# A transformer pair in split float32: where the SBUF buffers lie, with the two ends of the memory exchanged

## The chip, the cores and the metric

The kernel runs on 1 core of a Trainium2 chip. The metric is the time of one execution on the device, in microseconds. Before the change it is 1691.29 us, the median of 3 runs (1683.52 to 1696.0).

## What is computed

Two blocks run one after the other on 512 positions of width 1024, all in float32. The first block has three mixers side by side (an attention with forget gates of 8 heads, a windowed mean, a "stick-breaking" attention of 4 heads). The second block has two layers: a matrix memory (mLSTM) and an attention over a window of 128 with sinks, each followed by a layer norm, a squared-ReLU MLP, a layer norm and a gated side input. Cut to the MLP and the side input, in which the operands stand that this text is about:

```python
def squared_relu_mlp(x, w_up, w_down):
    return jnp.square(jax.nn.relu(x @ w_up)) @ w_down
...
        x = layer_norm(DEEPNORM_ALPHA * x + mix, mix_ln_g[i], mix_ln_b[i])
        x = layer_norm(DEEPNORM_ALPHA * x + squared_relu_mlp(x, mlp_w_up[i], mlp_w_down[i]), mlp_ln_g[i], mlp_ln_b[i])
        x = x + jax.nn.sigmoid(x @ ple_w_gate[i] + ple_b_gate[i]) * (p[i] @ ple_w_proj[i])
```

`w_up` is 1024 x 4096, `w_down` 4096 x 1024; the other weight matrices are 1024 wide as well.

## The kernel before

Activations lie transposed: features on the 128 partitions, the 512 positions along the free axis. A matrix of 1024 features is eight slices of 128 x 512 float32, that is 2048 bytes per partition and slice.

Every product with a weight matrix is made from halves. A number is split into a high part (rounded to the type `fp32r`) and the low rest, and three matmuls add up in one PSUM bank: high weight by high activation, low weight by high activation, high weight by low activation. The weights come in 238 blocks of 128 x 1024 float32 (4096 bytes per partition; the stationary operand of one matmul is a piece of 128 columns, 512 bytes per partition). For each block SyncE issues one DMA into `W_raw` (2 slots, L428), GpSimd writes `W_hi` (L445) and `W_lo` (L447), 4 slots each, and TensorE runs 8 x 3 matmuls with it. The inner lines of `product`, which all phases share, are

```python
pe.matmul(PS[:, bank, :], W_hi[:, slot, w], hi[:, kk, :], start=first, stop=False)      # L515
pe.matmul(PS[:, bank, :], W_lo[:, slot, w], hi[:, kk, :], start=False, stop=False)      # L516
done = pe.matmul(PS[:, bank, :], W_hi[:, slot, w], lo[:, kk, :], start=False, stop=last)  # L517
```

The second argument is the stationary operand (loaded by LDWEIGHTS, "PEld" in the profile), the third the moving one, 512 columns long. L485, L486 and L490 are the same three products in `weave`, with which some phases begin, and L825 to L827 are those of the small side product. The moving operand is one of three pairs:

- `A_hi`, `A_lo`: the split activations of 1024 features, in almost every phase;
- `H_hi`, `H_lo`: the 2048 hidden features of half an MLP, in the four `down` phases (8 tiles of 2 blocks each);
- `P_hi`, `P_lo`: the side input, in the two `proj` phases (8 tiles of a quarter block each).

The order of the work is written out by hand, engine by engine, with semaphores. ScalarE reads the banks out of PSUM (or VectorE does, for the residual sums in `X`), ScalarE writes the high parts and VectorE the low parts (`low_part`, L1297; `H_lo`, L1608). `GpSimd` may overwrite a weight slot when TensorE is done with it (the wait ahead of L444, a dummy operation on `HOLD`).

Buffers are allocated by `sb`, as on a stack. Each has a fixed byte address within the partition; those of a `with ... as part` or `sub` block are given back at its end, so that the buffers of the stages (`QK`, `MQK`, `QK3`, `H_hi`, `GATE` and so on) share their memory. Before the change the long-lived buffers are stacked from byte 16512 upwards in the order of the code, and the shared part stands above them, from 137760 up to 222432.

Of the kernel before, what the change touches and what calls it, by code (L numbers as in the profile page):

```python
# [19 lines left out]
F32 = mybir.dt.float32  # L20
F32R = mybir.dt.float32r
# [6 lines left out]
P = 128  # L28
T = 512
NT = T // P  # L30
D = 1024
KD = D // P
# [137 lines left out]

def build(nc, x, weights, constants, params, positions, ple_in, out):
    with ExitStack() as ctx:
        def sb(name, shape, dt=F32, where=ctx):
            return where.enter_context(nc.sbuf_tensor(name, shape, dt))

        def sem(name):
            return ctx.enter_context(nc.semaphore(name))


        X = sb("X", [P, KD, T])  # L180
        A_hi = sb("A_hi", [P, KD, T], F32R)
        A_lo = sb("A_lo", [P, KD, T], F32R)
        W_raw = sb("W_raw", [P, RAW_SLOTS, KD * P])
        W_hi = sb("W_hi", [P, W_SLOTS, KD * P], F32R)
        W_lo = sb("W_lo", [P, W_SLOTS, KD * P], F32R)
# [1703 lines left out]
```

## Time and profile before

| what | value |
|---|---|
| median of 3 runs | 1691.29 us |
| the profiled execution: its time, its span | 1691.69 us, 1689.5 us |
| TensorE busy | 1610.2 us, 95% of the span |
| GpSimd busy | 900.8 us, 53% |
| VectorE busy | 728.7 us, 43% |
| ScalarE busy | 424.5 us, 25% |
| mean DMA rate | 78 GB/s |
| mean granted TensorE clock | 0.987 of the full clock |

TensorE's busy time in this table is the union of matmuls whose ends are modelled, and one matmul's end lies behind the start of the next. How long TensorE takes for a matmul in a running stream is therefore read from the distance of two starts, or from a stretch of time divided by the number of matmuls in it, and not from the "mean ns" of a row. A stretch can lack some matmul records.

### The profile page before, as it was taken

What the parts mean: (1) busy time and instruction counts of PE and PEld (TensorE: products, weight loads), DVE (VectorE), ACT (ScalarE), POOL (GpSimd) and SP (SyncE); (2) the same over time, 40 slices, a digit from 0 to 9 for tenths busy, and PEclk for the clock granted to TensorE, in tenths of its full rate; (3) what the DMA queues carried; (4) which work ended last, traced back from release to release, by engine and by line L of the source; (5) the groups of instructions that cost most, each with busy time, mean ns of one, the idle gap of its engine ahead of it and who ended that gap; (6) DMA issues with size and microseconds to landing.
All of it is one profiled execution on the core that took longest, in us unless ns stands there. A gap on an engine that the chain in (4) does not pass through costs nothing.

```text
span 1689.5 us, 20635 instructions
## 1 busy us (share of the span) xinstructions
PE 1610.2 (95%) x7306; PEld 1280.2 (76%) x7306; DVE 728.7 (43%) x985; ACT 424.5 (25%) x916; POOL 900.8 (53%) x719
## 2 busy tenths in 40 slices
PE   5999998989999999999999999998999999999998
PEld 4788665778777778887888877777778888887876
DVE  5773243241103657500552154656576610453155
ACT  3321356221120132200220041147423200121041
POOL 4666300456542249766676646830156866676643
PEclk9999999999989999999999999999999999999999
DMA  4322100122311023332323213310022332333322
GB/s 156 100 88 88 62 1 13 53 85 94 93 50 50 13 88 100 100 100 88 100 91 108 90 59 100 100 51 0 13 88 75 104 96 90 97 100 100 99 76 75
DMA packets 36835, 132.34 MB, mean 78 GB/s; under 512 B 4105, under 2 KB 4385, under 8 KB 36770
## 3 DMA queue, kind: packets, MB, share of 16 engines
q1 hardware_dynamic: 35282, 128.23, 24.2%
q10 hardware_dynamic: 1488, 3.17, 0.5%
q8 instruction: 50, 0.82, 0.2%
q14 instruction: 15, 0.12, 0.0%
HBM read 129.26 MB, written 2.10 MB: 78 GB/s over the span
## 4 chain that ended last, share of the span: by engine, by line
PE 91%; ACT 3%; DVE 3%; issue 1%; DMA 1%; POOL 0%; SPq 0%; ACTq 0%; DVEq 0%; POOLq 0%
PE PS L515 23%; PE PS L517 23%; PE PS L516 23%; PE PS L485 2%; PE PS L490 2%; PE PS L486 2%; PE PS L630 2%; PE PS L601 2%; PE PS L770 1%; PE PS L617 1%; DMA W_raw<-in_weights 1%; ACT PR L1050 1%; PE PS L745 1%; PE PS L757 1%; PE PS L704 1%
## 5 line engine op out<-in xcount | busy, mean ns | idle before, releaser
L447 POOL TENSOR_TENSOR W_lo<-W_raw,W_hi 128x1024 fp32r<-128x1024 f32 x238 | 601.5, 2527 | 19.9
L515 PE MATMUL PS<-A_hi,W_hi 128*128 128x512 f32 x1176 | 468.0, 398 | 7.5 <-DVE A_lo L1297 3.7
L444 POOL TENSOR_TENSOR HOLD<-HOLD 1x1 f32<-1x1 f32 x238 | 60.2, 253 | 750.7 <-PE PS L517 458.8
L517 PE MATMUL PS<-A_lo,W_hi 128*128 128x512 f32 x1176 | 459.8, 391 | 0.0
L516 PE MATMUL PS<-A_hi,W_lo 128*128 128x512 f32 x1176 | 459.8, 391 | 0.0
L515 PEld LDWEIGHTS PS<-A_hi,W_hi 128*128 128x128 f32 x1176 | 222.1, 189 | 60.2 <-issue 8.6
L516 PEld LDWEIGHTS PS<-A_hi,W_lo 128*128 128x128 f32 x1176 | 222.2, 189 | 49.0 <-issue 3.6
L517 PEld LDWEIGHTS PS<-A_lo,W_hi 128*128 128x128 f32 x1176 | 221.8, 189 | 46.7
L445 POOL TENSOR_SCALAR W_hi<-W_raw 128x1024 fp32r<-128x1024 f32 x238 | 247.2, 1038 | 0.0
L515 PE MATMUL PS<-H_hi,W_hi 128*128 128x512 f32 x512 | 203.4, 397 | 2.7 <-ACT RELU L1180 2.7
L517 PE MATMUL PS<-H_lo,W_hi 128*128 128x512 f32 x512 | 203.0, 396 | 0.0
L516 PE MATMUL PS<-H_hi,W_lo 128*128 128x512 f32 x512 | 203.0, 396 | 0.0
L1608 DVE TENSOR_TENSOR H_lo<-SQR,H_hi 128x512 f32 (+1 forms) x64 | 122.4, 1913 | 57.4 <-ACT H_hi L1183 57.4
L1180 ACT ACTIVATE RELU<-PS 128x512 f32<-128x512 f32 x64 | 37.9, 592 | 322.2 <-PE PS L517 310.9
L1606 DVE TENSOR_TENSOR SQR<-RELU 128x512 f32<-128x512 f32 x64 | 81.3, 1270 | 85.9 <-ACT RELU L1180 85.9
L515 PEld LDWEIGHTS PS<-H_hi,W_hi 128*128 128x128 f32 x512 | 96.4, 188 | 27.8 <-ACT RELU L1180 4.4
L517 PEld LDWEIGHTS PS<-H_lo,W_hi 128*128 128x128 f32 x512 | 96.4, 188 | 23.5
L516 PEld LDWEIGHTS PS<-H_hi,W_lo 128*128 128x128 f32 x512 | 96.5, 188 | 23.3
L1555 DVE TENSOR_TENSOR X<-X,PS 128x512 f32<-128x512 f32 x32 | 22.0, 688 | 188.8 <-PE PS L517 188.8
L1552 DVE SCALAR_TENSOR_TENSOR X<-X,PS 128x512 f32<-128x512 f32 x24 | 16.4, 687 | 186.2 <-PE PS L517 177.6
L485 PE MATMUL PS<-A_hi,W_hi 128*128 128x512 f32 x168 | 69.2, 412 | 15.1 <-DVE MIX L1698 3.8
L1160 ACT ACTIVATE SQ<-X 128x512 f32<-128x512 f32 x28 | 17.7, 633 | 205.6 <-DVE X L1555 182.3
(247 smaller groups left out, 1807.5 us busy)
## 6 DMA issues: line engine op xcount, KB each, us to landing
W_raw<-in_weights SPq DMA_DIRECT2D x238, 512.0 KB, 3.5
X<-in_x SPq DMA_DIRECT2D x4, 512.0 KB, 6.1
out<-X ACTq DMA_DIRECT2D x8, 256.0 KB, 2.8
RELU<-in_ple_in ACTq DMA_DIRECT2D x2, 512.0 KB, 3.6
CONST<-in_constants SPq DMA_DIRECT2D x1, 913.5 KB, 10.8
PARAM<-in_params SPq DMA_DIRECT2D x1, 197.5 KB, 3.8
CONST<-in_constants SPq DMA_DIRECT2D x1, 192.0 KB, 7.6
NEG_C<-FF_PART ACTq DMA_DIRECT2D x3, 8.0 KB
```

Source lines behind the costliest of these rows:

```text
L444: pool.tensor_tensor(HOLD[:, 1 + s:2 + s], HOLD[:, 0:1], HOLD[:, 0:1], ALU.add)
L445: pool.tensor_scalar(W_hi[:, s, :], W_raw[:, r, :], 1.0, 1.0, ALU.mult, ALU.mult).then_inc(w_hi, 1)
L447: pool.tensor_tensor(W_lo[:, s, :], W_raw[:, r, :], W_hi[:, s, :].bitcast(F32), ALU.subtract).then_inc(w_lo, 1)
L485: pe.matmul(PS[:, i, :], W_hi[:, slot, w], hi[:, k, :], start=k == 0, stop=False)
L486: pe.matmul(PS[:, i, :], W_lo[:, slot, w], hi[:, k, :], start=False, stop=False)
L490: done = pe.matmul(PS[:, i, :], W_hi[:, slot, w], lo[:, k, :], start=False, stop=k == KD - 1)
L515: pe.matmul(PS[:, bank, :], W_hi[:, slot, w], hi[:, kk, :], start=first, stop=False)
L516: pe.matmul(PS[:, bank, :], W_lo[:, slot, w], hi[:, kk, :], start=False, stop=False)
L517: done = pe.matmul(PS[:, bank, :], W_hi[:, slot, w], lo[:, kk, :], start=False, stop=last)
L1180: act.activation(RELU[:, slot, :], bank, ACT.Relu).then_inc(by_act, 1)
L1606: dve.tensor_tensor(SQR[:, slot, :], RELU[:, slot, :], RELU[:, slot, :], ALU.mult).then_inc(h_sq, 1)
L1608: dve.tensor_tensor(H_lo[:, i, :], SQR[:, slot, :], H_hi[:, i, :].bitcast(F32), ALU.subtract).then_inc(h_lo, 1)
```

## The change

Long-lived buffers are no longer stacked from the bottom but from the top of the memory downwards (`side="right"`). The two exceptions are `A_hi` and `A_lo`, which are given `ctx` and so go to the left side, where they are now the lowest buffers; the shared part, on the left side as well, stands right above them.

```diff
-        def sb(name, shape, dt=F32, where=ctx):
-            return where.enter_context(nc.sbuf_tensor(name, shape, dt))
+        def sb(name, shape, dt=F32, where=None):
+
+            if where is None:
+                return ctx.enter_context(nc.sbuf_tensor(name, shape, dt, side="right"))
+            return where.enter_context(nc.sbuf_tensor(name, shape, dt, side="left"))
...
         X = sb("X", [P, KD, T])
-        A_hi = sb("A_hi", [P, KD, T], F32R)
-        A_lo = sb("A_lo", [P, KD, T], F32R)
+        A_hi = sb("A_hi", [P, KD, T], F32R, ctx)
+        A_lo = sb("A_lo", [P, KD, T], F32R, ctx)
```

No instruction is added, removed or moved: with the three new lines of code taken out of the count, the instruction lists of all five engines, with their operands' names and shapes, are the same row by row. What differs is the address in each operand. These are the start addresses that the allocation gives, in bytes within a partition, and the remainder of each by 64 (allocations start at multiples of 32; all slices of these buffers are multiples of 512 bytes long, so a slice has the remainder of its buffer):

```
buffer        before   mod 64     after   mod 64
X              16512      0      212960     32
A_hi           32896      0       16512      0
A_lo           49280      0       32896      0
W_raw          65664      0      204768     32
W_hi           73856      0      188384     32
W_lo           90240      0      172000     32
CONST         106624      0      163136      0
SUM           117088     32      159488      0
SQ            121184     32      153344      0
MIX           131424     32      143104      0
QK, H_hi      137760     32       49280      0
H_lo          170528     32       82048      0
RELU          203296     32      114816      0
P_hi          207392     32      118912      0
P_lo          211488     32      123008      0
```

The distance between moving and stationary operand changes too, by the same table: mod 64 it is 0 before for `A` with `W` and 32 for `H` and `P` with `W`; after, it is 32 for all three pairs.

## Rows read from the trace of the kernel before

**Rows 1.** The page: its first line and its part 1.
```profile
span 1689.5 us, 20635 instructions
PE 1610.2 (95%) x7306; PEld 1280.2 (76%) x7306; DVE 728.7 (43%) x985; ACT 424.5 (25%) x916; POOL 900.8 (53%) x719
```
**Rows 2.** Stretches: start:end and length in us, then each engine's busy us (instructions).
```profile
799.00:885.00 86.00, 86.00 (x380) 71.20 (x380) 44.85 (x30) 20.02 (x45) 61.26 (x47) 1.00 0.29 93
887.00:976.00 89.00, 89.00 (x381) 71.54 (x381) 18.15 (x22) 6.29 (x11) 58.14 (x47) 1.00 0.32 99
1442.00:1529.00 87.00, 86.59 (x382) 71.75 (x383) 45.40 (x31) 20.01 (x45) 61.96 (x47) 1.00 0.30 94
1530.00:1620.00 90.00, 89.60 (x383) 72.06 (x383) 18.35 (x22) 6.63 (x12) 58.81 (x48) 1.00 0.32 99
```
**Rows 3.** Timeline of PE in an `up` phase, the ten matmuls between 833.8 and 836.0.
```profile
833.80 0.39 PE L516 MATMUL PS<-A_hi,W_lo 128*128 128x512 f32 x1
...
835.84 0.39 PE L516 MATMUL PS<-A_hi,W_lo 128*128 128x512 f32 x1
```
**Rows 4.** Timeline in a `down` phase: start, length, engine, instruction.
```profile
724.72 0.40 PE L515 MATMUL PS<-H_hi,W_hi 128*128 128x512 f32 x1
724.72 0.19 PEld L516 LDWEIGHTS PS<-H_hi,W_lo 128*128 128x128 f32 x1
724.95 0.39 PE L516 MATMUL PS<-H_hi,W_lo 128*128 128x512 f32 x1
...
726.83 0.39 PE L515 MATMUL PS<-H_hi,W_hi 128*128 128x512 f32 x1
```
**Rows 5.** Groups of instructions by form: xcount | busy us, mean ns | idle before.
```profile
L515 PE MATMUL PS<-A_hi,W_hi 128*128 128x512 f32 x1176 | 468.0, 398 | 7.5 <-DVE A_lo L1297 3.7 <-issue 1.7 <-ACT MG L1115 0.8
L485 PE MATMUL PS<-A_hi,W_hi 128*128 128x512 f32 x168 | 69.2, 412 | 15.1 <-DVE MIX L1698 3.8 <-ACT A_hi L1168 3.7 <-POOL W_lo L447 3.1
L515 PE MATMUL PS<-H_hi,W_hi 128*128 128x512 f32 x512 | 203.4, 397 | 2.7 <-ACT RELU L1180 2.7
L825 PE MATMUL PS<-P_hi,W_hi 128*128 128x512 f32 x32 | 13.2, 411 | 0.0
```
**Rows 6.** Timeline of PE in the `qk1` phase behind a float32 matmul (L575), eight matmuls.
```profile
50.90 0.40 PE L516 MATMUL PS<-A_hi,W_lo 128*128 128x512 f32 x1
...
52.52 0.39 PE L517 MATMUL PS<-A_lo,W_hi 128*128 128x512 f32 x1
```
**Rows 7.** Groups by form: weight loads, with stationary operands at 0 and at 32 mod 64.
```profile
L516 PEld LDWEIGHTS PS<-A_hi,W_lo 128*128 128x128 f32 x1176 | 222.2, 189 | 49.0 <-issue 3.6
L516 PEld LDWEIGHTS PS<-H_hi,W_lo 128*128 128x128 f32 x512 | 96.5, 188 | 23.3
L630 PEld LDWEIGHTS PS<-V,PT 128*128 128x128 f32 x384 | 50.4, 191 | 2.1 <-ACT PT L1039 0.2
L601 PEld LDWEIGHTS PS<-QK,STAGE_Q 128*128 128x128 f32 x192 | 29.6, 194 | 5.3 <-ACT STAGE_Q L1023 2.4 <-issue 1.7 <-DVE V L1401 1.0
```
**Rows 8.** The weights' way: groups on POOL, a wait of POOL (timeline), the DMA's landing (page, part 6).
```profile
L447 POOL TENSOR_TENSOR W_lo<-W_raw,W_hi 128x1024 fp32r<-128x1024 f32 x238 | 601.5, 2527 | 19.9
L445 POOL TENSOR_SCALAR W_hi<-W_raw 128x1024 fp32r<-128x1024 f32 x238 | 247.2, 1038 | 0.0
724.96 0.18 POOL L444 TENSOR_TENSOR HOLD<-HOLD 1x1 f32<-1x1 f32 x1 [1.88 <-PE PS L517]
W_raw<-in_weights SPq DMA_DIRECT2D x238, 512.0 KB, 3.5
```
**Rows 9.** The page's part 4: the chain that ended last, by engine.
```profile
PE 91%; ACT 3%; DVE 3%; issue 1%; DMA 1%; POOL 0%; SPq 0%; ACTq 0%; DVEq 0%; POOLq 0%
```
**Rows 10.** Groups by form on ACT and DVE: one operation with sources at different remainders.
```profile
L929 ACT ACTIVATE A_hi<-MIX 128x512 fp32r<-128x512 f32 x16 | 10.1, 633 | 19.6 <-DVE MIX L1362 11.8 <-DVE MIX L1698 7.7
L929 ACT ACTIVATE A_hi<-X 128x512 fp32r<-128x512 f32 x16 | 9.2, 623 | 52.0 <-PE PS L517 41.8 <-DVE X L1626 10.3
L1542 DVE TENSOR_TENSOR PS<-PS,SQ 128x512 f32<-128x512 f32 x24 | 16.7, 698 | 0.0
L1561 DVE TENSOR_TENSOR PS<-PS,X 128x512 f32<-128x512 f32 x20 | 14.0, 699 | 0.7
```

## The prediction

> **What bounds the kernel now.** I read the page first, for which engine fills the span. TensorE is busy for 1610.2 of 1689.5 us [rows 1], and 91% of the chain that ended last is TensorE's, with 3% each for ScalarE and VectorE [rows 9]. So the kernel takes as long as its stream of matmuls, plus some 79 us in which TensorE has none (1689.5 - 1610.2). Since the change alters nothing but addresses, the next question is whether the trace holds the same instruction at two kinds of address, and whether it runs differently there. For TensorE it does. The view of stretches has the `up` phases, whose moving operand is `A`, beside the `down` phases, whose moving operand is `H`; count and shape of the matmuls are the same (384 in each phase, 128 x 512), and the granted clock is 1.00 in all four. An `up` stretch holds 380 matmuls in 86 us and 382 in 87 us, a `down` stretch 381 in 89 us and 383 in 90 us [rows 2]: about 227 ns against 234 ns. The timelines say it without the edges. In `up` ten matmuls start between 833.80 and 835.84, nine distances of 226.7 ns [rows 3]. In `down` ten start between 724.72 and 726.83 (L515 to L515, nine distances), 234.4 ns each [rows 4]. So a matmul on `H` costs 7.7 ns more than one on `A`.
>
> Work on the other engines is no explanation: VectorE has 44.85 us of work in the faster stretch and 18.15 in the slower one, ScalarE 20.02 and 6.29, GpSimd 61.26 and 58.14 [rows 2]. What is left, by the code and the table of addresses, is the moving operand's place: `A` starts at 0 mod 64 and below byte 65664, `H` at 32 mod 64 and above byte 137760. The stationary operand, `W`, is the same in both.
>
> **The change part by part.** No instruction, wait or DMA is added or moved, so each term is a duration that may differ.
>
> *Moving operands H and P.* Both go from 32 to 0 mod 64, and from above 137760 to below 127104. Whether remainder or region is the cause of the 7.7 ns, the new place has what `A` has now. L515 runs 512 times on `H` and L825 32 times on `P` [rows 5], each one of three matmuls for a slice: 3 x (512 + 32) = 1632 matmuls. 1632 x 7.7 ns = 12.6 us less, all of it on the path, since TensorE runs without a gap there (89.00 busy of 89.00 [rows 2]). The bounds are 0 (the cause is neither) and 12.6.
>
> *Moving operand A.* It moves down by 16384 bytes and keeps its remainder: no cost.
>
> *Stationary operands W_hi and W_lo.* They go from 0 to 32 mod 64 and to the top of the memory. No row before shows an `fp32r` stream with the stationary operand in such a place, so this cost has to be bounded. From below it is zero: the weight load of the next matmul starts together with the running one (724.72 both) and takes 0.19 us of the 0.23 that it has [rows 4], and it is as long in the slow stretches as in the fast ones, 188 and 189 ns [rows 7], so its length does not set the distance. Loads of stationary operands that lie at 32 mod 64 and high now (`PT`, `STAGE_Q`) take 191 and 194 ns [rows 7], 2 to 5 ns longer, which still ends ahead of the next matmul. From above there are two ways. If the distance did follow the load, 5 ns on all 3 x (1176 + 168 + 512 + 32) = 5664 matmuls [rows 5] would be 28 us. If what makes `H` slow is not the moving operand's own place but its place relative to `W` (mod 64, or the half of the memory), then `A` would stand to `W` as `H` does now: 3 x (1176 + 168) = 4032 matmuls [rows 5] times 7.7 ns, 31.0 us more, and nothing gained on `H` and `P`. I take zero, because the only difference that the trace shows lies with the moving operand, four times as long as the stationary one and so the stream for which an extra access is likeliest to count. That is a choice between ends far apart, and the range keeps both. A warning stands in the trace: behind a float32 matmul in `qk1`, matmuls on `A` too run slowly for a moment, eight starts from 50.90 to 52.52, 231 ns each [rows 6], at addresses that are fast elsewhere. So the time depends on how the two streams fall against each other as well, and not on the moving address alone.
>
> *The weights' way.* DMA, `W_raw`, and GpSimd's two operations get other addresses. Their durations are 1.04 and 2.53 us, the DMA lands in 3.5, a block lasts 24 x 0.227 = 5.4 us on TensorE, and GpSimd waited 1.88 us for TensorE ahead of this block [rows 8]. Cover of 1.9 us a block hides anything up to half again of GpSimd's work; were the cover gone, each further 0.1 us would cost 238 x 0.1 = 24 us. I cost it at nothing.
>
> *ScalarE and VectorE.* `X` goes to 32 mod 64; `SQ`, `SUM`, `MIX` and the stages' buffers go to 0. The same activation reads `MIX` (32 now) in 633 ns and `X` (0 now) in 623; the same addition reads `SQ` (32) in 698 and `X` (0) in 699 [rows 10]. At most 1.6%, on 6% of the span (3% and 3% [rows 9], 101 us), with gains and losses both: within 1.6 us. I take 0.
>
> *Weighing a rule.* The only difference in rows between operands of one shape is 226.7 against 234.4 ns [rows 3, 4]. The Trainium skill, in "SBUF — State Buffer", section "Door 1: The DMA port swizzle", speaks of cachelines of 16 bytes; a start at 32 mod 64 is as good as one at 0 by it. The same page, section "Who interferes with whom", gives TensorE two independent read ports and has it wait for nobody. By these rules addresses that are multiples of 32 are alike, and the sum would be 0 instead of -12.6 us. The trace does not agree that all places are alike; which property of a place counts, it does not say.
>
> The sum is 1691.7 - 12.6 = 1679.1 us. It is made against the profiled execution, 1691.69 us (span 1689.5), and the median of the runs shown is 1691.29, the same to 0.4 us.
>
> **The rivals.** *Forecast, chance 0.42:* the moving operand's own place decides, the `down` and `proj` phases run at 226.7 ns, 1679 us (1675 to 1685 with the side terms).
>
> *The stationary operand's place counts too, chance 0.34; it ends slower.* Every `up`, `gate`, `out` phase on `A` goes to about 234 ns, and `H` stays or gets better by little. For: the disturbed stretch in `qk1` [rows 6], and that after the change moving and stationary operand differ mod 64 everywhere, as they do now only where it is slow. Against: equal weight loads in slow and fast stretches [rows 7]. Price: +31.0 us and no gain, 1723 us; 1710 if `H` gets its gain all the same (1691.7 + 31.0 - 12.6). It decides from 12.6 us / 4032 = 3.1 ns more per matmul on `A` on: above that the change is no gain.
>
> *Nothing to measure, chance 0.16:* the cause is something else that `H` and `P` share and keep, or gain and a small loss on `W` (2.2 ns on 5664 matmuls) cancel. 1692 us, 1686 to 1698. This is also what the page's rules above would make of it, with no gain in `down`.
>
> *The side engines or the weights' way, chance 0.08:* half of it a gain beyond the forecast (VectorE and ScalarE faster on stage buffers in the 79 us where TensorE waits, to some 1672 us), half of it a loss of GpSimd's cover, 1715 us and more.
>
> **How the numbers follow.** The predicted time is that of the likeliest, 1679 us. Its own range is 1675 to 1685. Cases of both signs are likely, so the range reaches from a little beyond the forecast to the second rival with a few microseconds for runs, 1672 to 1727; it leaves out some 0.1. About 1% is what a measurement of this kernel can tell from no change, 17 us: below 1674 counts as faster, above 1708 as slower. The forecast, -0.7%, is within it. Faster: 0.04 from the side engines and 0.03 from the forecast's lower edge in the runs' spread, 0.07. Slower: 0.33, of the second rival all but its mildest forms (0.30) and 0.03 of the last. Within 1%: 0.60.
>
> **What would show it.** In the profile after, each step has its stretch. The distance of starts in `down` (in either MLP) is 226.7 ns if the first term is right, 234 if not. The distance in `up` stays 226.7 if the stationary operand's place is free, and goes to 230 or more if it is not. The count of matmuls in an 86 us stretch tells the same. GpSimd's two operations keep 1.04 and 2.4 to 2.5 us and its wait ahead of a block stays near 1.9 us. The gaps of TensorE stay near 79 us in all. The prediction is wrong, if not in its sum then in its reason, when `down` keeps its 234 ns, and wrong in its sign when `up` leaves 226.7.

## The result, and the profile after

The kernel is slower: 1722.19 us (median of 6 runs, 1721.17 to 1723.34) against 1690.93 us for the kernel before (6 runs, 1683.52 to 1696.00), a ratio of 1.0192 with a 95% interval of 1.0168 to 1.0217. The profiled execution took 1722.04 us, its span is 1719.9 us, 30.4 more than before.

The page of the kernel after (its first line, part 1, the chain's shares by engine) answers to [rows 1] and [rows 9]:

```profile
span 1719.9 us, 20635 instructions
PE 1640.9 (95%) x7306; PEld 1284.9 (75%) x7306; DVE 721.7 (42%) x985; ACT 424.8 (25%) x916; POOL 900.2 (52%) x719
PE 92%; ACT 3%; DVE 3%; issue 1%; DMA 1%; POOL 0%; SPq 0%; ACTq 0%; DVEq 0%; POOLq 0%
```

TensorE's busy time grew by 30.7 us (1640.9 - 1610.2), as much as the span; ScalarE and GpSimd did the same work in the same time, and VectorE in 7.0 us less (721.7 against 728.7). The stretches of a `down` and of an `up` phase, each 86 us long, answer to [rows 2]:

```profile
725.00:811.00 86.00, 86.00 (x369) 69.13 (x368) 7.00 (x9) 0.73 (x2) 54.93 (x46) 1.00 0.30 92
816.00:902.00 86.00, 86.00 (x369) 69.13 (x368) 43.36 (x29) 19.63 (x45) 59.02 (x46) 1.00 0.30 92
```

Before, 86 us of `up` held 380 matmuls; now they hold 369, as many as `down`. The first and the last of the 384 matmuls of this `up` phase in the timeline give the distance to a few hundredths of a nanosecond:

```profile
815.22 0.47 PE L518 MATMUL PS<-A_hi,W_hi 128*128 128x512 f32 x1 [0.83 <-issue]
...
905.03 0.39 PE L520 MATMUL PS<-A_lo,W_hi 128*128 128x512 f32 x1
```

(905.03 - 815.22) / 383 = 234.49 ns. All times per matmul below are worked out in this way (227.0 ns or less is a fast stream), from the first and last start of a phase. They are taken from the four `down` phases and from the two of the four `up` phases that follow on a `down` phase; the other two begin with waits for a layer norm. The first step of a phase is longer than the rest (0.31 us here), which adds 0.2 ns to each of these averages. Before, the same phase had 226.9 ns and `down` 234.55; after, `down` has 234.54. So `A` lost its fast rate and `H` gained nothing: 4032 matmuls on `A` by 7.6 ns are 30.6 us, the whole difference of the spans.

The loads and the side engines, in the view of groups by form, answer to [rows 7], [rows 8] and [rows 10]:

```profile
L519 PEld LDWEIGHTS PS<-A_hi,W_lo 128*128 128x128 f32 x1176 | 223.0, 190 | 56.3 <-issue 3.6
L450 POOL TENSOR_TENSOR W_lo<-W_raw,W_hi 128x1024 fp32r<-128x1024 f32 x238 | 602.4, 2531 | 19.9
L448 POOL TENSOR_SCALAR W_hi<-W_raw 128x1024 fp32r<-128x1024 f32 x238 | 247.5, 1040 | 0.0
L932 ACT ACTIVATE A_hi<-MIX 128x512 fp32r<-128x512 f32 x16 | 10.1, 631 | 20.3 <-DVE MIX L1365 11.8 <-DVE MIX L1701 8.4
L932 ACT ACTIVATE A_hi<-X 128x512 fp32r<-128x512 f32 x16 | 9.2, 622 | 53.5 <-PE PS L520 43.2 <-DVE X L1629 10.3
L1545 DVE TENSOR_TENSOR PS<-PS,SQ 128x512 f32<-128x512 f32 x24 | 16.7, 698 | 0.0
```

The durations here are within 1% of their values before, though `X`, `SQ` and `MIX` changed their remainder by 64 and GpSimd's buffers moved across the memory. A weight load took 189 ns and takes 190.

### The profile page after: what moved, and what is told of

Its sections match the earlier page's. It is cut to its first block, busy times and chain, and to the rows that moved or that the text cites. A ratio compares the mean times of both kernels' runs of the same rounds, so it can differ in the third digit from the quotient of the medians.

```text
span 1719.9 us, 20635 instructions
## 1 busy us (share of the span) xinstructions
PE 1640.9 (95%) x7306; PEld 1284.9 (75%) x7306; DVE 721.7 (42%) x985; ACT 424.8 (25%) x916; POOL 900.2 (52%) x719
## 4 chain that ended last, share of the span: by engine, by line
PE 92%; ACT 3%; DVE 3%; issue 1%; DMA 1%; POOL 0%; SPq 0%; ACTq 0%; DVEq 0%; POOLq 0%
PE PS L518 23%; PE PS L519 23%; PE PS L520 23%; PE PS L488 2%; PE PS L489 2%; PE PS L493 2%; PE PS L633 2%; PE PS L604 2%; PE PS L773 1%; PE PS L620 1%; DMA W_raw<-in_weights 1%; ACT PR L1053 1%; PE PS L760 1%; PE PS L707 1%; PE PS L670 1%
## 5 line engine op out<-in xcount | busy, mean ns | idle before, releaser
L518 PE MATMUL PS<-A_hi,W_hi 128*128 128x512 f32 x1176 | 476.5, 405 | 7.5 <-DVE A_lo L1300 3.7
L519 PE MATMUL PS<-A_hi,W_lo 128*128 128x512 f32 x1176 | 468.4, 398 | 0.0
L520 PE MATMUL PS<-A_lo,W_hi 128*128 128x512 f32 x1176 | 468.0, 398 | 0.0
L447 POOL TENSOR_TENSOR HOLD<-HOLD 1x1 f32<-1x1 f32 x238 | 58.4, 246 | 780.7 <-PE PS L520 481.3
L1609 DVE TENSOR_TENSOR SQR<-RELU 128x512 f32<-128x512 f32 x64 | 80.1, 1252 | 99.2 <-ACT RELU L1183 99.2
L488 PE MATMUL PS<-A_hi,W_hi 128*128 128x512 f32 x168 | 71.8, 427 | 15.0 <-DVE MIX L1701 3.8
L489 PE MATMUL PS<-A_hi,W_lo 128*128 128x512 f32 x168 | 70.5, 420 | 0.0
```

Source lines behind the costliest of these rows:

```text
L447: pool.tensor_tensor(HOLD[:, 1 + s:2 + s], HOLD[:, 0:1], HOLD[:, 0:1], ALU.add)
L488: pe.matmul(PS[:, i, :], W_hi[:, slot, w], hi[:, k, :], start=k == 0, stop=False)
L489: pe.matmul(PS[:, i, :], W_lo[:, slot, w], hi[:, k, :], start=False, stop=False)
L1609: dve.tensor_tensor(SQR[:, slot, :], RELU[:, slot, :], RELU[:, slot, :], ALU.mult).then_inc(h_sq, 1)
```

## The experiments

What is in question is which property of the addresses sets the time from the start of one `fp32r` matmul to the start of the next. In this part a distance in ns is this time, and a distance in bytes is one between two addresses. Only addresses differ between the kernels that follow; all compute the whole reference. In the stretches quoted for them the granted clock is 1.00 (the third value from the right).

**The remainder by 64, first four kernels.** By theory "difference" a matmul is slow where moving and stationary operand have different remainders by 64, by "either" where one of the two is at 32, and by "halves" where one of them lies in the lower and the other in the upper part of the memory.

```diff
 # e1_after_plus32_top: the kernel after, with
+        PAD_TOP = sb("PAD_TOP", [P, 8])
         X = sb("X", [P, KD, T])
 # e2_before_part_plus32: the kernel before, with
+        PAD_PART = sb("PAD_PART", [P, 8])
         with ExitStack() as part:
             QK = sb("QK", [P, 8, T], F32, part)
 # e3_all_plus32: the kernel before, with
+        PAD_LOW = sb("PAD_LOW", [P, 8])
         X = sb("X", [P, KD, T])
 # e4_all_at_32: PAD_LOW and PAD_PART together
```

> Kernel after, with one buffer of 32 bytes allocated first from the top: every long-lived buffer moves down by 32 bytes, so W_hi and W_lo lie at 0 mod 64, as A, H and P do, and still at the top of the memory (188352 and 171968). Theory 'difference' (a matmul of the fp32r stream is slow, 234.4 ns from start to start, where moving and stationary operand have different remainders by 64, and fast, 226.7 ns, where they are equal): all 5664 matmuls fast, up and down at 226.7 ns, 1679 us. Theory 'either' (slow where one of the two is at 32 mod 64): the same, 1679 us. Theory 'halves' (slow where moving and stationary operand lie in different halves of the memory): all slow as in the kernel after, 1722 us.

Measured: 1716.57 us, ratio to before 1.0155 (1.0124 to 1.0185). `down` 233.6 ns, `up` 233.5.

> Kernel before, with 32 bytes allocated ahead of the shared part: H and P lie at 0 mod 64, as A and W do, and still high (137792 and up), with W low. 'Difference' and 'either': down and proj go to 226.7 ns, 1679 us. 'Halves': down stays at 234.4 ns, 1691 us.

Measured: 1690.91 us, ratio 1.0003 (0.9987 to 1.0019). `down` 233.6, `up` 226.9. The two stretches, `down` and `up`:

```profile
704.00:790.00 86.00, 86.00 (x370) 69.28 (x369) 7.07 (x9) 0.73 (x2) 55.37 (x46) 1.00 0.30 93
795.00:881.00 86.00, 86.00 (x381) 71.05 (x379) 45.28 (x30) 20.02 (x45) 60.64 (x46) 1.00 0.30 92
```

> Kernel before, with 32 bytes allocated ahead of everything: A and W both lie at 32 mod 64, H and P at 0. 'Difference': up stays at 226.7 ns (32 and 32), down stays at 234.4 (0 and 32), 1691 us. 'Either': all at 234.4 ns, 1722 us. 'Halves': as before, 1691 us.

Measured: 1691.28 us, ratio 1.0002 (0.9988 to 1.0016). `down` 234.55, `up` 226.9.

> Kernel before, with 32 bytes ahead of everything and 32 more ahead of the shared part: A, W, H and P all lie at 32 mod 64. 'Difference': all at 226.7 ns, 1679 us. 'Either': all at 234.4 ns, 1722 us. 'Halves': 1691 us.

Measured: 1693.15 us, ratio 1.0013 (0.9999 to 1.0028). `down` 233.6, `up` 226.9.

Both theories on the remainder by 64 fall with e1, e2 and e4: there moving and stationary operand have the same remainder and the stream is slow all the same. "Either" falls a second time with e3 and e4, where `A` and `W` at 32 modulo 64 are fast. "Halves" was left, with a small puzzle beside it: an equal remainder by 64 was worth 0.9 ns (233.6 against 234.55).

**Sides, and single pairs.** Four kernels went after a border in the memory.

```diff
 # f1_a_high_too: the kernel after, with
-        A_hi = sb("A_hi", [P, KD, T], F32R, ctx)
-        A_lo = sb("A_lo", [P, KD, T], F32R, ctx)
+        A_hi = sb("A_hi", [P, KD, T], F32R)
+        A_lo = sb("A_lo", [P, KD, T], F32R)
 # f2_a_w_low: the kernel after, with
-        W_hi = sb("W_hi", [P, W_SLOTS, KD * P], F32R)
-        W_lo = sb("W_lo", [P, W_SLOTS, KD * P], F32R)
+        W_hi = sb("W_hi", [P, W_SLOTS, KD * P], F32R, ctx)
+        W_lo = sb("W_lo", [P, W_SLOTS, KD * P], F32R, ctx)
 # f3_a0_w32_low: the kernel before, with
+        PAD_W = sb("PAD_W", [P, 8])
         W_raw = sb("W_raw", [P, RAW_SLOTS, KD * P])
 # f5_w_lo_alone_high: the kernel before, with
-        W_lo = sb("W_lo", [P, W_SLOTS, KD * P], F32R)
+        W_lo = ctx.enter_context(nc.sbuf_tensor("W_lo", [P, W_SLOTS, KD * P], F32R, side="right"))
```

> Kernel after, with A_hi and A_lo at the top like the other long-lived buffers: A (180192 to 212960) and W (139232 to 172000) both lie above byte 131072, H and P (16512 and up) below. Theory 'same side' (a matmul of the fp32r stream is fast, 226.7 ns from start to start, where moving and stationary operand lie on the same side of a border near byte 131072, slow, 233.6 to 234.5 ns, where they do not): up at 226.7, down and proj at 234.5, 1691 us. Theory 'either high' (slow where one of the two lies above the border): all at 234, 1722 us.

Measured: 1693.28 us, ratio 1.0012 (0.9999 to 1.0025). `up` 226.9, `down` 234.55, as "same side" has it.

> Kernel after, with W_hi and W_lo on the left side behind A: A at 16512 to 49280, W at 49280 to 82048, H_hi at 82048 to 114816, H_lo at 114816 to 147584, everything else long-lived at the top. By both theories A stays fast, H_hi becomes fast in all 16 slices, and H_lo in the 7 of 16 slices that lie wholly below 131072: in down L518 and L519 (H_hi; as numbered in that kernel) at 226.7 ns, L520 (H_lo) at 226.7 for slices 0 to 6 and 234 from slice 8 on. 512 x 2 + 512 x 7/16 = 1248 matmuls x 7.6 ns = 9.5 us less than before, 1682 us. Were the border at 114688 (half of 229376), all of H_lo would be slow: 1024 x 7.6 = 7.8 us less. If the time depends on the distance of the two operands, H_hi slices near W are faster than those far from it.

Measured: 1681.28 us, ratio 0.9929 (0.9913 to 0.9944). The time was the expected one and the reason was not: `down` has 227.0 ns in every phase, and the slices of `H_lo` above byte 131072 are as fast as those below. The stretches of `down` and `up`:

```profile
708.00:794.00 86.00, 86.00 (x381) 71.20 (x380) 7.30 (x9) 0.73 (x2) 56.62 (x47) 1.00 0.31 94
796.00:882.00 86.00, 86.00 (x381) 71.18 (x380) 45.00 (x30) 20.06 (x45) 61.13 (x47) 1.00 0.29 93
```

> Kernel before, with 32 bytes allocated between A and W: A at 0 mod 64, W at 32, both low. The remainder was seen to cost 0.9 ns per matmul where the operands lie on different sides (234.5 against 233.6). If it costs as much on the same side, up goes to 227.6 ns and the kernel to 1695 us; if it costs something only there where the stream is slow already, up stays at 226.7 and the kernel at 1691 us.

Measured: 1716.23 us in one run, against 1691.12 for the kernel before. A miss for both expectations: with `W` moved by 32 bytes away from `A`, and both still low, `up` goes from 226.9 to 233.5 ns.

```profile
720.00:806.00 86.00, 86.00 (x369) 69.16 (x368) 7.22 (x9) 0.73 (x2) 54.82 (x46) 1.00 0.31 94
811.00:897.00 86.00, 86.00 (x370) 69.28 (x369) 43.28 (x29) 19.73 (x45) 59.24 (x46) 1.00 0.30 92
```

That ends "halves": 32 bytes on one side of any border do nearly what the exchange did. What sorts all phases so far is the distance from stationary to moving operand modulo a power of two. `A_hi` minus `W_hi` is 32896 - 73856, a multiple of 512, in the kernel before; in f2 both `A` and `H` are at a multiple of 512 from `W`; in the kernel after, `A` is at 16512 - 188384, which is 160 modulo 512.

> Kernel before, with W_lo alone at the top of the memory (212960) and W_hi left low (73856). In the phases on A two of three matmuls have both operands low; L516 has W_lo. If a matmul is slow for its own pair of operands, the distance from L516 to the next start is 234 and the others stay at 226.7. If it is slow while the load of the next stationary operand reads from the other side, it is the distance from L515 to L516 (L515 runs while W_lo is loaded). Either way some 7.6 x 1344 = 10 us more in the phases on A.

Measured: 1706.92 us in one run, 15.8 more than the kernel before (1691.12), where some 10 were expected. `up` 232.8 ns on average, and, against both expectations, none of the three distances stays fast: the averages over the phase are 231.6 from L515 to L516, 232.7 from L516 to L517, 233.3 from L517 to L515. One of three weight loads at a bad distance (`W_lo`, 160 modulo 256 from `A`) costs three quarters of what three do (5.9 of 7.6 ns), and all three steps pay, so the penalty does not stay with the single pair. The question whether it is the own load or the one of the next matmul stays open.

**Distance modulo.** The last four kernels test that alone.

```diff
 # g1_after_plus352_top: the kernel after, with
+        PAD_TOP = sb("PAD_TOP", [P, 88])
         X = sb("X", [P, KD, T])
 # g2_before_part_plus96: the kernel before, with
+        PAD_PART = sb("PAD_PART", [P, 24])
         with ExitStack() as part:
 # g3_h_at_128_256_384_64 and g4_h_at_32_16_4_96: as g2, and
+H_OFFSETS = [32, 64, 96, 16]     # elements; g4: [8, 4, 1, 24]
...
-            H_hi = sb("H_hi", [P, HALF_FF, T], F32R, part)
-            H_lo = sb("H_lo", [P, HALF_FF, T], F32R, part)
+            H_hi_all = sb("H_hi", [P, HALF_FF * T + 128], F32R, part)
+            H_lo_all = sb("H_lo", [P, HALF_FF * T + 128], F32R, part)
+            def at_offset(buffer, elements):
+                return buffer[:, elements:elements + HALF_FF * T].rearrange("p (i t) -> p i t", t=T)
+            H_hi = [at_offset(H_hi_all, e) for e in H_OFFSETS]
+            H_lo = [at_offset(H_lo_all, e) for e in H_OFFSETS]
...
-                    product(f"down{l}{letter}", H_hi, H_lo, h_lo, HALF_FF * (2 * l + half))
+                    product(f"down{l}{letter}", H_hi[2 * l + half], H_lo[2 * l + half], h_lo, HALF_FF * (2 * l + half))
```

> Kernel after, with 352 bytes allocated first from the top: W_hi is at 188032, W_lo at 171648, still at the far end of the memory from A (16512) and H (49280), but now at a distance from every moving operand that is a multiple of 512 bytes. Theory 'distance modulo' (the fp32r stream is fast, 226.7 ns, where moving and stationary start differ by a multiple of M bytes, M one of 128, 256, 512, wherever they lie): all 5664 matmuls fast, 1679 us. Any theory of sides, halves or heights in the memory: slow as in the kernel after, 1717 to 1722 us.

Measured: 1679.67 us, ratio 0.9934 (0.9909 to 0.9959). This is the kernel after with nothing changed but 352 unused bytes at the top, and it is 42.5 us faster than that. `W` lies 139 to 172 thousand bytes from `A`. `down` and `up`:

```profile
709.00:795.00 86.00, 86.00 (x381) 71.16 (x379) 6.82 (x9) 0.73 (x2) 56.25 (x46) 1.00 0.29 92
797.00:883.00 86.00, 86.00 (x381) 71.20 (x380) 45.17 (x30) 20.05 (x45) 60.80 (x46) 1.00 0.31 92
```

> Kernel before, with 96 bytes allocated ahead of the shared part: H_hi at 137856, 64000 = 125 x 512 bytes above W_hi. 'Distance modulo': down and proj at 226.7 ns, 12.4 us less than before, 1679 us. Theories of place: 1691 us.

Measured: 1679.23 us, ratio 0.9924 (0.9901 to 0.9946), the fastest version of this study beside g1. First and last matmul of the first `down` phase, and the stretch:

```profile
707.37 0.50 PE L517 MATMUL PS<-H_hi,W_hi 128*128 128x512 f32 x1 [0.69 <-ACT RELU L1182]
...
794.31 0.39 PE L519 MATMUL PS<-H_lo,W_hi 128*128 128x512 f32 x1
```

```profile
708.00:794.00 86.00, 86.00 (x381) 71.22 (x380) 7.20 (x9) 0.73 (x2) 56.51 (x46) 1.00 0.30 94
```

(794.31 - 707.37) / 383 = 227.0 ns, where [rows 2] and [rows 4] had 234.4.

> As the kernel before with the shared part up by 96 bytes; H is put at a distance of 128, 256, 384 and 64 bytes (modulo 512) from W in the four down phases in turn. M = 128: the first three at 226.7 ns, the fourth at 233.6. M = 256: the second at 226.7, the others slow. M = 512: all four slow. P and A stay fast.

Measured: 1687.08 us in one run. The four `down` phases, in the order 128, 256, 384, 64 bytes:

```profile
709.00:795.00 86.00, 86.00 (x372) 69.74 (x371) 7.00 (x9) 0.74 (x2) 55.54 (x46) 1.00 0.31 93
887.00:973.00 86.00, 86.00 (x381) 71.19 (x380) 17.64 (x22) 6.29 (x11) 57.80 (x47) 1.00 0.32 101
1351.00:1437.00 86.00, 86.00 (x372) 69.74 (x371) 6.95 (x9) 0.75 (x2) 55.59 (x46) 1.00 0.30 93
1529.00:1615.00 86.00, 86.00 (x377) 70.59 (x376) 17.64 (x22) 6.29 (x11) 57.99 (x47) 1.00 0.34 100
```

Only 256 is fast (381 matmuls in 86 us); 128 and 384 are equal to each other and slow (232.7 ns). So the unit is 256 bytes. The phase at 64 bytes takes 229.2 ns, where 233.6 were expected.

> As g3, with distances of 32, 16, 4 and 96 bytes in the four down phases. Seen so far: 234.5 ns where the distance is 32 modulo 128, 233.6 where it is 64, 233.5 where it is 96. The first and fourth repeat these; 16 and 4 bytes are new. If a line of 16 bytes is the unit, 16 costs as 32 does (234) and 4 costs more; if only the phase of two streams by 128 bytes counts, 4 and 16 bytes may cost less, in proportion.

Measured: 1690.00 us in one run. The four phases, 32, 16, 4 and 96 bytes:

```profile
708.00:794.00 86.00, 86.00 (x370) 69.11 (x369) 7.45 (x9) 0.74 (x2) 55.26 (x47) 1.00 0.31 95
887.00:973.00 86.00, 86.00 (x373) 69.81 (x372) 17.56 (x22) 6.31 (x11) 57.24 (x46) 1.00 0.32 100
1350.00:1436.00 86.00, 86.00 (x365) 68.20 (x364) 7.50 (x9) 0.75 (x2) 54.26 (x46) 1.00 0.31 94
1530.00:1616.00 86.00, 86.00 (x370) 69.22 (x369) 17.99 (x22) 6.30 (x11) 56.62 (x47) 1.00 0.34 101
```

4 bytes cost most, 236.9 ns, and 16 cost less than 32, 232.0 ns: neither expectation holds for both. 32 and 96 are at 233.6 both; I had taken 234.5 for 32 from kernels in which the distance is 160 modulo 256, not 32.

All kernels, put together by the distance from stationary to moving start modulo 256 (only streams in which `W_hi` and `W_lo` have the same distance, so without f5):

```
distance mod 256   ns per matmul     seen in
      0            226.9 to 227.0    A in before, e2, e3, e4, f1; A and H in f2, g1, g2; H in g3 (256)
      4            236.9             H in g4
     16            232.0             H in g4
     32            233.6             H in g4
     64            229.2             H in g3
     96            233.6             H in g4
    128            232.7             H in g3, twice (128 and 384)
    160            234.5             H in before, e3, f1, f3; A and H in after
    192            233.5 to 233.6    A and H in e1; H in e2, e4
    224            233.5             A in f3
```

One number sorts the `down` and the two uninterrupted `up` phases of all these thirteen kernels: no two of them with the same distance differ by more than 0.2 ns, be the operands low, high, near or far, and the remainder of the addresses themselves is free (`A` and `W` at 128, 160 or 224 modulo 256 are equally fast in before, e3 and f1).

**The other engines as a cause.** GpSimd writes into `W_hi` and `W_lo`, and a DMA into `W_raw`, while TensorE reads. A clash of the moving operand's reads with these writes could sort the phases in the same way. For `W_raw` f2 rules it out: there it stayed at 204768, which is 160 modulo 256 from `A` and from `H`, and both are fast. For GpSimd the traces do. In the first `down` phase of the kernel before, GpSimd is idle for the 1.88 us ahead of 724.96 [rows 8], and VectorE and ScalarE have no instruction in that stretch. The matmuls in it:

```profile
723.08 0.40 PE L517 MATMUL PS<-H_lo,W_hi 128*128 128x512 f32 x1
...
724.72 0.40 PE L515 MATMUL PS<-H_hi,W_hi 128*128 128x512 f32 x1
```

Seven distances, (724.72 - 723.08) / 7 = 234.3 ns: no faster than the rest. Over the whole phase, the steps with all three engines idle average 234.2 ns (114 of them) and those with GpSimd at work 234.3 (221); steps with and without DMA packets under way differ as little, 234.2 and 234.3. In the phase at 4 bytes of g4 the two kinds are at 236.6 both.

## Why the prediction was wrong

**What bounds the kernel, and where:** right. The path is TensorE's stream, `A` runs at 227 ns and `H` at 234, the moving operand's place was what differed, and the other engines had no part in it.

**The gain on H and P, 12.6 us:** this term failed. I took it for granted that if `A`'s place (0 mod 64, low) is good, `H` in such a place is good. The property that counts is not one of the moving operand's place at all. `H` stood at 160 modulo 256 from `W` before, and stands at 160 after: 234.55 and 234.54 ns, 0 us gained. That it kept exactly this number is chance. The size was right for the case in which the distance is mended: g2, with `H` moved by 96 bytes, has 11.9 us less (1679.23 against 1691.17 for the kernel before in the runs beside it), and its span 13.2 us less (1689.5 - 1676.3), against 1632 x 7.5 ns = 12.3.

**The stationary operand's place, taken at 0:** this is the term that turned the sign. The upper bound that I had worked out, 31.0 us for 4032 matmuls on `A` whose relation to `W` becomes `H`'s, is what came: 30.4 us in the spans, 1722 us against 1723. The reason that I gave for zero, that the load of 188 ns takes as long in the slow stretches as in the fast ones, was true and proves nothing. The load's length does not change, and the stream still depends on where the load reads relative to the moving operand (f3: `W` moved by 32 bytes, loads as before, 6.6 ns more per matmul). The warning that I had seen, matmuls on `A` slow for eight starts behind a float32 matmul [rows 6], is not this effect: in g2, where every `fp32r` pair is at a distance of 0, the same eight starts lie between 50.51 and 52.13, 231.4 ns each, before the stream is fast again. What slows them was not looked into. The table of addresses had the answer's form in it, the distance mod 64, but I looked at remainders by 64 alone; with 256 the two cases that the trace has are 0 and 160, and the changed kernel's 160 for `A` and for `H` can be worked out before any run.

**The rival that ends slower** (chance 0.34) had the result in place, price and time: `up` at 234, `H` unchanged, 1723 us. It was right about the relation and wrong about its kind: neither "mod 64" nor "half of the memory" is it.

**The weights' way and the side engines at nothing:** right. GpSimd's operations took 1.04 and 2.53 us as before, its wait ahead of a block grew rather than shrank (481.3 us in all against 458.8 for L447, L444 before), and ScalarE's busy time moved by 0.3 us (424.5 to 424.8). VectorE's fell by 7.0 us, more than the 1.6 us that I had allowed for both engines: the 64 operations `SQR<-RELU` went from 1270 to 1252 ns, and the rest are a few early operations of which single ones changed by up to 2 us (`ANG`, `ROWS`, `QK`), in both directions. None of it shows in the span, which grew by what TensorE's matmuls explain.

```profile
POOL HOLD L447 <- PE PS L520: 481.3, 182, 95.9
```

**The rule that was weighed.** The Trainium skill, "SBUF — State Buffer", section "Door 1: The DMA port swizzle", gives cachelines of 16 bytes. The trace of the kernel before did not agree that multiples of 32 are alike, and the runs show why it could not: a distance of 16 bytes costs 5 ns a matmul, 32 cost 6.7, and 256 nothing. By the same page of the Trainium skill, section "Who interferes with whom", TensorE's two read ports are independent; the trace does not agree: with `A` where it was, new addresses of the weights move its stream by 6.6 ns a matmul (f3), though each load still takes 189 ns. By that view of no difference the forecast would have been 1691 us.

**What stays open:** which structure has the period of 256 bytes, whether a matmul suffers from its own load or from the next one (f5 had all three distances slow), and why 64 bytes cost only a third of what 32 and 96 cost. The three steps of a slice are not alike there: at 64 bytes they average 225.8, 229.2 and 231.7 ns, at 96 bytes 231.0, 231.0 and 238.0, while at 32 and 160 they are equal to 0.5 ns. No run here tells why.

## What to carry to other kernels

Where a stream of `fp32r` matmuls with a new stationary operand for each is the bound, start moving and stationary buffers at a distance that is a multiple of 256 bytes (shown for a stationary operand of 128 x 128 and a moving one of 128 x 512; no other shape was tried), and check the distances after each new buffer: an unused pad of 96 bytes made this kernel 0.76% faster, and 352 bytes took the exchanged one from 1722 to 1680 us. When one instruction form runs at two speeds in one trace, list the addresses of all its operands and their differences, not only those of the operand whose name differs; and two good placements found by eye (0 mod 64, low) are a guess until one pad has been moved.

## What was not expected of the hardware

- The distance modulo 256 bytes between moving and stationary operand sets the rate of the `fp32r` stream, 226.9 ns at 0 and up to 236.9 ns at 4 bytes. The place in the memory does not count in these runs: operands 139 thousand bytes apart are as fast as neighbours (g1).
- The runs of one kernel differ by up to 12 us (1683.52 to 1696.00 for the kernel before). The mean granted clock goes with the time: 0.991 in the run of 1684.01 us and 0.983 in that of 1695.78 (the kernel before, beside g1). One place where the clock differs can be seen in the traces. TensorE waits in a layer norm, and then the stream starts at half or at full clock. Stretches of g1 (three) and of e2 (two) around the same place, with the granted clock third from the right:

```profile
608.00:617.00 9.00, 5.59 (x29) 4.04 (x27) 6.38 (x13) 1.77 (x4) 3.54 (x3) 0.77 0.40 117
617.00:623.00 6.00, 5.78 (x14) 4.55 (x15) 6.00 (x11) 5.38 (x8) 0.00 (x0) 0.50 0.00 0
623.00:629.00 6.00, 6.00 (x28) 4.98 (x27) 5.19 (x9) 5.45 (x8) 0.00 (x0) 0.99 0.00 0
```

```profile
606.00:615.00 9.00, 5.87 (x29) 4.02 (x27) 6.51 (x13) 1.79 (x4) 3.54 (x3) 0.81 0.40 117
615.00:621.00 6.00, 5.79 (x25) 4.74 (x26) 6.00 (x11) 5.39 (x8) 0.00 (x0) 1.00 0.00 0
```

TensorE was busy for 5.59 of the 9 us before in the one and for 5.87 in the other. In g1 the next 6 us were granted 0.50 of the clock (1.2 of 2.4 GHz) and held 14 matmuls, in e2 1.00 and 25: 11 matmuls or 2.5 us for one such place. I read the spread of the runs from such places; that all of it comes from them was not shown.
